# First attention: the value products with their operands exchanged, results by rows and turned back per pair of heads

## The chip, the cores and the metric

The kernel runs on one core of one Trainium2 chip. The metric is the device time of one execution in microseconds. TensorE (PE) multiplies and transposes into PSUM, VectorE (DVE), ScalarE (ACT) and GpSimd (POOL) work element by element, and SyncE (SP) issues the transfers. Each engine runs its own instructions in order; between engines there are semaphores.

## What is computed

The program computes two transformer blocks for 1024 rows of width 1024. The change is in the attention of the first block, which breaks a stick for each query instead of taking a softmax. Cut to what matters:

```python
def stick_breaking_attention(q, k, v):          # 16 heads of 64 columns
    for i in range(seq // Q_BLOCK):             # 8 blocks of 128 queries
        q0, kend = i * Q_BLOCK, (i + 1) * Q_BLOCK
        z = einsum('bhqd,bhkd->bhqk', q[q0:kend], k[:kend]) * inv_sqrt_d
        mask = kpos < qpos
        log_beta = log_sigmoid(z)
        log_1m_beta = where(mask, log_beta - z, 0.0)
        suffix = lax.cumsum(log_1m_beta, axis=3, reverse=True) - log_1m_beta
        a = where(mask, exp(log_beta + suffix), 0.0)
        outs.append(einsum('bhqk,bhkd->bhqd', a, v[:kend]))
...
    o = o.transpose(0, 2, 1, 3).reshape(b, s, D_ATTN)
    o = o * jax.nn.silu(z)                      # the gate
    return x + gate[:, None, :] * (o @ w_out)
```

Everything is fp32. Large products and the scores are made from high and low parts rounded to fp32r; the transposes and the products of `a` with the values are plain fp32.

## The kernel before

The work of the first attention is 128 items, 16 heads times 8 query blocks, in the order 6, 7, 0, 1, 4, 5, 2, 3 of blocks within each head (`STICK_ORDER`). Item n with query block i has i+1 key blocks, so its tiles are up to 1024 wide. The engines pass items on at fixed distances; the loops over steps are written out for each engine (`stick_pe` L748, `stick_act` L984, `stick_dve` L1103, `stick_pool` L1580):

- TensorE makes the scores of item n (L764, L765, two passes of fp32r for every 512 columns, and the mask at L767) in PSUM banks 0 to 3.
- ScalarE takes the sigmoid into `beta` (L994) and the sigmoid of the negative in place (L996), VectorE scans that product from the right into `rest` (L1120, a tile of `M` or `rest`), POOL multiplies the two (L1601): that is `a`, queries by keys, in `beta`.
- Four steps later (`TURN_LAG`) TensorE turns `a` block by block (L779) in pieces of up to four blocks, alternately in PSUM banks 4 and 5; a piece waits for the copy of the piece two places before it. ScalarE copies each piece into `a_T` (L1008), after the two sigmoids of its step. `a_T[i // 2]` holds two items, i-1 and i, side by side.
- Seven steps later (`VALUE_LAG`) come the value products (L801). The values of one head are stationary, 128 keys by 128 columns, of which the 64 columns of the other head of the pair are zero; the moving operand is `a_T`, for both items of a couple at once, 256 columns, and 128 in the last block. So only the odd items have value products, and these are halved over two steps (`part`). The result stands columns by queries, for both heads of a pair, in banks 6 and 7: the zeros let the second head add to the first.
- After an odd head VectorE multiplies each half of 512 queries with the gate `sz` into `s_o` (L1110), and POOL rounds it to the two parts of `opA` (L1587, L1590) for the next product, units from `U_BOUT`.
- SP loads per head its keys and queries (`hin`) and its 64 columns of values (`head_v`, L1348). POOL zeroes the other columns once (L1577).

What decides when a transposed piece may go on:

```python
c = STICK_PLACE[n, p]
if c >= 2:
    pe.wait_ge(act_done, at("stick_hi", c - 2))
```

Of the kernel before, what the change touches and what calls it, by code (L numbers as in the profile page):

```python
# [16 lines left out]
P = 128  # L17
# [118 lines left out]

TURN_LAG, VALUE_LAG, OUT_LAG = 4, 7, 9
BETAS, FACTORS = 5, 3
# [40 lines left out]
STICK_PIECES = stick_pieces()  # L179
STICK_PLACE = {piece: c for c, piece in enumerate(STICK_PIECES)}  # L180

# [111 lines left out]
def program(nc, a, out, known):  # L293
# [3 lines left out]
    with ctx:  # L297
# [10 lines left out]
        def at(name, offset, shape, dt=F32):  # L308
            return nc.alloc_sbuf_tensor_at(name, [P] + shape, dt, offset=offset)
# [36 lines left out]
               [at("a_T3", AT_X + 16 * KIB, [4, 2 * P]), at("a_T3b", AT_X + 20 * KIB, [4, 2 * P])]]  # L346
        head_v = [at(f"head_v{i}", AT_B + (44 + 16 * i) * KIB, [T]) for i in range(2)]
        s_o = at("s_o", AT_M + 12 * KIB, [2, HALF])
        ident_r = at("ident_r", AT_M + 16 * KIB, [P], F32R)
        mask_r = at("mask_r", AT_M + 16 * KIB + 512, [P], F32R)  # L350
# [383 lines left out]

        def stick_kbs(c):
            n, p = STICK_PIECES[c]
            return range(NQ * p, min(NQ * p + NQ, stick_item(n)[1] + 1))
# [10 lines left out]
        def stick_pe(pe):  # L748
            def scores(n):
# [20 lines left out]
                step(pe_done, "stick_s", n)  # L770

            def turn(n):
                pe.wait_ge(pool_done, at("stick_a", n))
                for p in range(stick_item(n)[1] // NQ + 1):
                    c = STICK_PLACE[n, p]
                    if c >= 2:
                        pe.wait_ge(act_done, at("stick_hi", c - 2))
                    for kb in stick_kbs(c):
# [3 lines left out]
                    step(pe_done, "stick_T", c)  # L782

            def values(n, part):

                h, i = stick_item(n)
                s, o = h % 2, 6 + i // NQ
                q0 = (i - 1) % NQ * P
                middle = (i + 1) // 2 - (i > NQ)

                if part == 0:
                    if n % NT == 1:
                        pe.wait_ge(value_in[s], at("value_in", h))
                    if n == 1:
                        pe.wait_ge(pool_done, at("head_zero"))
                    pe.wait_ge(act_done, at("stick_hi", STICK_PLACE[n, i // NQ]))
                    if h >= 2 and h % 2 == 0 and i in (1, NT - 1):
                        pe.wait_ge(dve_done, at("stick_o", h // 2 - 1, i // NQ))
                for kb in range(i + 1)[slice(middle, None) if part else slice(0, middle)]:
                    cols_of = slice(P if kb == i else 0, 2 * P)  # L800
                    ins = pe.matmul(PS[:, o, q0 + cols_of.start:q0 + 2 * P], head_v[s][:, kb * P:(kb + 1) * P],  # L801
                                    a_T[i // 2][kb // NQ][:, kb % NQ, cols_of],
                                    start=(h % 2 == 0 and i in (1, NT - 1) and kb == 0), stop=(h % 2 == 1 and kb == i),
                                    skip_group_check=True)
                if part:
                    ins.then_inc(pe_done, 1)
                    step(pe_done, "stick_v", n)
# [4 lines left out]
            for n in range(STICK_ITEMS + VALUE_LAG + 1):  # L812
                if n < STICK_ITEMS:
                    scores(n)
                if n > VALUE_LAG:
                    part = (n - VALUE_LAG) % 2 == 0
                    values(n - VALUE_LAG - part, part)
# [166 lines left out]
        def stick_act(act):  # L984
            for n in range(STICK_ITEMS + OUT_LAG + 1):
                if n < STICK_ITEMS:
                    w = (stick_item(n)[1] + 1) * P
                    z = stick_z(n)
                    act.wait_ge(pe_done, at("stick_s", n))
                    if n == 0:  # L990
                        act.wait_ge(x_out, at("x_out", 0))
                    if n >= BETAS:
                        act.wait_ge(pe_done, at("stick_T", STICK_PLACE[n - BETAS, stick_item(n - BETAS)[1] // NQ]))
                    act.activation(beta[n % BETAS][:, 0:w], z, ACT.Sigmoid).then_inc(act_done, 1)  # L994
                    step(act_done, "stick_beta", n)
                    act.activation(z, z, ACT.Sigmoid, scale=-1.0).then_inc(act_done, 1)  # L996
                    step(act_done, "stick_rest", n)
                m = n - TURN_LAG
                if 0 <= m < STICK_ITEMS:
                    for p in range(stick_item(m)[1] // NQ + 1):  # L1000
                        c = STICK_PLACE[m, p]
                        kbs = stick_kbs(c)
                        act.wait_ge(pe_done, at("stick_T", c))
                        if m >= NT:
                            act.wait_ge(pe_done, at("stick_v", (m - NT) | 1))
# [3 lines left out]
                        step(act_done, "stick_hi", c)  # L1009

# [92 lines left out]
        def stick_dve(dve):  # L1103
            def finish(j, hf, n):

                dve.wait_ge(pe_done, at("stick_v", n))
                dve.wait_ge(reader(U_BOUT - 1), at("free", U_BOUT - 1))
                if j:
                    dve.wait_ge(pool_done, at("stick_out", j - 1, hf))
                dve.tensor_tensor(s_o[:, hf, :], PS[:, 6 + hf, :], sz[:, j, hf * HALF:(hf + 1) * HALF],  # L1110
                                  ALU.mult).then_inc(dve_done, 1)
                step(dve_done, "stick_o", j, hf)

            for n in range(STICK_ITEMS + OUT_LAG + 1):
                if n < STICK_ITEMS:
# [134 lines left out]
        def _(sp):  # L1250
# [73 lines left out]
            def head_loads(h):  # L1324
# [20 lines left out]
                if h >= 2:  # L1345
                    sp.wait_ge(pe_done, at("stick_v", NT * (h - 1) - 1))
                parts_of = "p (b s d) -> p b s d"
                sp.dma_start(head_v[s][:].rearrange(parts_of, b=NT, s=2)[:, :, s, :],  # L1348
                             v_dram[h // 2].rearrange(parts_of, b=NT, s=2)[:, :, s, :]).then_inc(value_in[h % 2], 16)
                step(value_in[h % 2], "value_in", h, by=16)  # L1350

# [153 lines left out]
        def _(pool):  # L1505
# [46 lines left out]
            def stick_consts():  # L1552
# [16 lines left out]
                step(pool_done, "stick_consts")  # L1569
                for u in (U_QZ + KC - 1, U_QZ + KC - 2):  # L1570
                    pool.wait_ge(stored[u % 2], at("stored", u))
                for u in (U_KV + 2 * KC - 1, U_KV + 2 * KC - 2):
                    pool.wait_ge(v_stored[u % 2], at("v_stored", u))
                for e in range(2):
                    other = head_v[e][:].rearrange("p (b s d) -> p b s d", b=NT, s=2)[:, :, 1 - e, :]
                    pool.wait_ge(pool_done, now(pool_done))
                    pool.memset(other, 0.0).then_inc(pool_done, 1)  # L1577
                    step(pool_done, "head_zero")

            def stick_pool():  # L1580
# [13 lines left out]

                for n in range(STICK_ITEMS + OUT_LAG + 1):
                    if n < STICK_ITEMS:
# [5 lines left out]
                        step(pool_done, "stick_a", n)  # L1602
                    e = n - OUT_LAG
                    if 0 <= e < STICK_ITEMS and e % NT in (5, 7) and e // NT % 2:
                        finish(e // NT // 2, stick_item(e)[1] // NQ)

# [1601 lines left out]
```

## Time and profile before

| | us |
|---|---|
| median of 3 runs | 2759.29 (2758.49 to 2763.61) |
| the profiled execution, own time | 2765.38 |
| its span, first to last instruction | 2763.6 |
| TensorE busy in the span | 2596.2 |
| first attention, first scores to last value product | some 930 to 1211 |

TensorE records are its passes. Their ends are modelled and overlap, so the distance between starts tells what a pass costs. PEld are weight loads. In the timeline one row can hold several equal instructions (x6); its length goes from the first start to the last end. "[0.33 <-PE PS L767]" is idle time before the row and what ended it.

### The profile page before, as it was taken

To read this page: it belongs to the slowest core of one execution; us is meant where nothing else is said; L and a number is where in the kernel's file an instruction comes from. 1 tells how busy PE (TensorE), PEld (TensorE's weight loads), DVE (VectorE), ACT (ScalarE), POOL (GpSimd) and SP (SyncE) were. 2 spreads that over 40 slices of the span, in tenths; PEclk is the share of its full clock that TensorE was granted. 3 is DMA by queue.
4 is the path that set the end of the run, shared out by engine and by line. 5 is a ranking of instruction groups with operands and counts; after the bars stand their busy time and mean duration, and the time that the engine had idled before them with its cause. 6 is when DMAs were issued, how large, how long until landed. Compare 5 with 4: busy or idle time off the path is not lost.

```text
span 2763.6 us, 34691 instructions
## 1 busy us (share of the span) xinstructions
PE 2596.2 (94%) x12363; PEld 2160.0 (78%) x12363; DVE 1548.8 (56%) x2099; ACT 1110.7 (40%) x1866; POOL 855.5 (31%) x626
## 2 busy tenths in 40 slices
PE   3899999999999999999899998789997999999998
PEld 2688888788778799987788877678875888887887
DVE  5666665641325466657764437775568777771112
ACT  3400001431411488856643437661265555551000
POOL 1233332012233466630132220233102323225664
PEclk7999999999999999999999999999999999999999
DMA  5244444344166544434253337414242333339933
GB/s 217 82 147 138 137 137 122 98 155 135 69 230 193 139 111 110 111 116 151 84 183 130 107 125 178 157 44 168 77 145 76 107 107 107 122 98 301 295 91 123
DMA packets 377272, 374.81 MB, mean 136 GB/s; under 512 B 36323, under 2 KB 284556, under 8 KB 376972
## 3 DMA queue, kind: packets, MB, share of 16 engines
q1 hardware_dynamic: 346844, 303.91, 37.0%
q10 hardware_dynamic: 30256, 68.69, 6.6%
q8 instruction: 99, 1.62, 0.2%
q14 instruction: 73, 0.60, 0.1%
HBM read 286.55 MB, written 85.98 MB: 135 GB/s over the span
## 4 chain that ended last, share of the span: by engine, by line
PE 75%; DVE 13%; ACT 5%; DMA 4%; issue 1%; POOL 1%; SPq 0%; ACTq 0%; DVEq 0%; POOLq 0%
PE PS L1743 27%; PE PS L1828 22%; PE PS L1897 8%; PE PS L801 5%; PE PS L779 2%; DMA mod_raw<-in_w_ada 2%; PE PS L1810 2%; PE PS L1787 1%; PE PS L765 1%; PE PS L764 1%; DVE opBf L2938 1%; DVE M L2599 1%; PE PS L1942 1%; DVE prob L1176 1%; ACT opBf L2085 1%
## 5 line engine op out<-in xcount | busy, mean ns | idle before, releaser
L1743 PE MATMUL PS<-opA,w_hi 128*128 128x512 f32 x2240 | 703.9, 394 | 12.2 <-POOL w_lo L1549 5.9
L1743 PEld LDWEIGHTS PS<-opA,w_hi 128*128 128x128 f32 x2240 | 425.2, 190 | 102.9 <-issue 7.3
L1743 PE MATMUL PS<-opA,w_lo 128*128 128x512 f32 x1120 | 439.8, 393 | 0.0
L1544 POOL CAST w_hi<-w_raw 128x1024 fp32r<-128x1024 f32 (+1 forms) x118 | 123.0, 1043 | 770.0 <-PE PS L1743 450.7
L1828 PE MATMUL PS<-opB,Xr 128*128 128x512 f32 x1120 | 308.7, 393 | 15.9 <-ACT M L2264 15.3
L1549 POOL TENSOR_TENSOR w_lo<-w_raw,w_hi 128x1024 fp32r<-128x1024 f32 (+1 forms) x120 | 290.8, 2424 | 83.6 <-ACT w_hi L2144 74.1
L1828 PE MATMUL PS<-opA,Xr 128*128 128x512 f32 x980 | 279.0, 395 | 6.5 <-DVE M L2955 3.4
L2599 DVE SCALAR_TENSOR_TENSOR M<-mod_raw,small,M 128x512 f32<-128x512 f32 x168 | 175.2, 1043 | 169.9 <-DMA mod_raw<-in_w_ada 85.3
L1828 PEld LDWEIGHTS PS<-opB,Xr 128*128 128x128 f32 x1120 | 212.1, 190 | 62.2 <-ACT M L2264 16.6
L1743 PEld LDWEIGHTS PS<-opA,w_lo 128*128 128x128 f32 x1120 | 212.6, 190 | 44.1 <-issue 0.2
L1828 PEld LDWEIGHTS PS<-opA,Xr 128*128 128x128 f32 x980 | 184.0, 190 | 51.1 <-ACT M L2264 8.0
L2881 DVE SCALAR_TENSOR_TENSOR X<-PS,mod,X 128x512 f32<-128x512 f32 x64 | 48.0, 750 | 296.8 <-PE PS L1897 207.1
L1828 PE MATMUL PS<-opA,w_first 128*128 128x512 f32 x840 | 198.0, 392 | 7.4 <-ACT M L2274 7.4
L1828 PEld LDWEIGHTS PS<-opA,w_first 128*128 128x128 f32 x840 | 158.9, 189 | 41.0 <-ACT M L2274 7.8
L1717 POOL TENSOR_TENSOR X<-w_raw 128x512 f32<-128x512 f32 x36 | 48.4, 1345 | 382.8 <-DVE xn L2669 229.3
L1743 PE MATMUL PS<-opB,w_hi 128*128 128x512 f32 x512 | 159.9, 391 | 2.4 <-DVE opB L2869 1.4
L1120 DVE TENSOR_TENSOR_SCAN M<-PS,beta 128x896 f32<-128x896 f32 (+7 forms) x86 | 116.4, 1359 | 71.3 <-ACT PS L996 59.8
L2955 DVE TENSOR_TENSOR M<-M,PS 128x512 f32<-128x512 f32 x140 | 96.2, 687 | 100.5 <-ACT M L2264 65.2
L2919 DVE TENSOR_TENSOR Xr<-X,Xr 128x512 fp32r<-128x512 f32 x140 | 116.0, 829 | 63.3 <-ACT Xr L2236 55.3
L1897 PE MATMUL PS<-opA,w_hi 128*128 128x512 f32 x480 | 149.3, 389 | 0.0
L2158 ACT ACTIVATE squares<-X 128x512 f32<-128x512 f32 x48 | 30.4, 633 | 232.1 <-DVE X L2881 228.4
L2264 ACT ACTIVATE M<-PS 128x512 f32<-128x512 f32 x105 | 62.8, 598 | 151.3 <-PE PS L1828 132.5
(256 smaller groups left out, 4737.7 us busy)
## 6 DMA issues: line engine op xcount, KB each, us to landing
mod_raw<-in_w_ada SPq DMA_DIRECT2D x96, 256.0 KB, 2.9
z_dram<-opB ACTq DMA_DIRECT2D x44, 512.0 KB, 3.9
w_raw<-in_a_w_in SPq DMA_DIRECT2D x32, 512.0 KB, 4.9
hin<-q_dram SPq DMA_DIRECT2D x64, 256.0 KB, 5.8
w_raw<-in_w_down SPq DMA_DIRECT2D x32, 512.0 KB, 4.2
opA<-z_dram SPq DMA_DIRECT2D x60, 256.0 KB, 5.2
mod_raw<-in_b_mod_w SPq DMA_DIRECT2D x48, 256.0 KB, 2.8
X<-x_dram SPq DMA_DIRECT2D x24, 512.0 KB, 6.2
```

The source lines that it names most:

```text
L779: ins = pe.transpose(PS[:, 4 + c % 2, (kb - NQ * p) * P:(kb - NQ * p + 1) * P], beta[n % BETAS][:, kb * P:(kb + 1) * P], ident[:])
L801: ins = pe.matmul(PS[:, o, q0 + cols_of.start:q0 + 2 * P], head_v[s][:, kb * P:(kb + 1) * P], a_T[i // 2][kb // NQ][:, kb % NQ, cols_of], ...
L1120: dve.tensor_tensor_scan(rest[n % FACTORS][:, 0:w][:, ::-1], stick_z(n)[:, ::-1], beta[n % BETAS][:, 0:w][:, ::-1], 1.0, ALU.mult, ALU.byp ...
L1544: pool.tensor_copy(hi, raw).then_inc(pool_done, 1)
L1549: pool.tensor_tensor(lo, raw, hi.bitcast(F32), ALU.subtract).then_inc(pool_done, 1)
L1743: ins = pe.matmul(ps, w[:, k0 + k, :], rhs(part, k0 + k), start=(k == 0 and n == 0), stop=(k == chunks - 1 and n == 2))
L1828: ins = pe.matmul(PS[:, seven_bank(i, which), :], seven_weight(q, i, which, w)[:, c * P:(c + 1) * P], token_part(which, part, c), start=(s ...
L1897: ins = pe.matmul(PS[:, down_bank(hf, n), :], w[:, s, k, :], z_operand(hf, g, part, k), start=(g == 0 and k == 0 and m == 0), stop=(g == 2 ...
L2264: act.activation(block_tile(q, i, 1)[:, 0:HALF] if n == 2 else M[1][:, n * HALF:(n + 1) * HALF], PS[:, seven_bank(i, P1), :], ACT.Copy).th ...
L2599: dve.scalar_tensor_tensor(out=acc, in0=mod_raw[:, n % 2, :], scalar=c, in1=acc, op0=ALU.mult, op1=ALU.add).then_inc(dve_done, 1)
L2919: dve.tensor_tensor(seven_weight(q, i, which, 1), seven_source(i, which), seven_weight(q, i, which, 0).bitcast(F32), ALU.subtract).then_in ...
L2955: dve.tensor_tensor(tile[:, hf * HALF:(hf + 1) * HALF], former, PS[:, seven_bank(i, which), :], ALU.add).then_inc(dve_done, 1)
```

## The change

- The value products exchange their operands (L801 before, L830 after): the turned weights of one item, 128 keys by 128 queries, are stationary, and the 64 value columns of the head move. Every item has its own products, i+1 of them, in one step at the lag of 7. The result stands queries by columns in bank 6 for the even head and bank 7 for the odd, 64 columns for each query block.
- The values need no zeros: they are loaded for two heads at once into `pair_v`, and POOL's two memsets go.
- After each head VectorE copies its bank into `rows_o` (L1150, `ROWS_LAG` 8). After an odd head TensorE turns the pair back (`turn_back`, L842, `BACK_LAG` 9): four transposes for the upper half of the queries, and in the next step four for the lower half. These take places in the rotation of banks 4 and 5 (`STICK_TURNS`), so `turn_free` makes the piece two places behind them wait for VectorE.
- VectorE's gate product then reads bank 4 or 5 (L1158) and comes at `OUT_LAG` 10 and 11, behind the scan of that step; POOL's output follows at the same lag. The loops run one step longer.

```diff
-TURN_LAG, VALUE_LAG, OUT_LAG = 4, 7, 9
+TURN_LAG, VALUE_LAG, ROWS_LAG, BACK_LAG, OUT_LAG = 4, 7, 8, 9, 10
...
+def pair_done(t, lag):
+
+    for hf in (1, 0):
+        h = head_done(t - lag - (1 - hf))
+        if h is not None and h % 2:
+            return h // 2, hf
+    return None
+
+def stick_turns():
+
+    turns = []
+    for t in range(STICK_ITEMS + OUT_LAG + 2):
+        n = t - TURN_LAG
+        if 0 <= n < STICK_ITEMS:
+            turns += [("a", n, p) for p in range(stick_item(n)[1] // NQ + 1)]
+        if pair_done(t, BACK_LAG):
+            turns.append(("o",) + pair_done(t, BACK_LAG))
+    return turns
...
+            def turn_free(c):
+
+                if c >= 2 and STICK_TURNS[c - 2][0] == "o":
+                    pe.wait_ge(dve_done, at("stick_o", *STICK_TURNS[c - 2][1:]))
+                elif c >= 2:
+                    pe.wait_ge(act_done, at("stick_hi", *STICK_TURNS[c - 2][1:]))
...
-                for kb in range(i + 1)[slice(middle, None) if part else slice(0, middle)]:
-                    cols_of = slice(P if kb == i else 0, 2 * P)
-                    ins = pe.matmul(PS[:, o, q0 + cols_of.start:q0 + 2 * P], head_v[s][:, kb * P:(kb + 1) * P],
-                                    a_T[i // 2][kb // NQ][:, kb % NQ, cols_of],
...
+                if h >= 2 and n % NT == 0:
+                    pe.wait_ge(dve_done, at("stick_rows", h - 2))
+                for kb in range(i + 1):
+                    ins = pe.matmul(PS[:, 6 + s, i * DH:(i + 1) * DH],
+                                    a_T[i // 2][kb // NQ][:, kb % NQ, n % 2 * P:n % 2 * P + P],
+                                    pair_v[j % 2][:, kb, s, :], start=(kb == 0), stop=(kb == i), skip_group_check=True)
...
+            def turn_back(j, hf):
+
+                c = STICK_PLACE["o", j, hf]
+                turn_free(c)
+                pe.wait_ge(dve_done, at("stick_rows", 2 * j + 1))
+                for b in range(NQ):
+                    ins = pe.transpose(PS[:, 4 + c % 2, b * P:(b + 1) * P],
+                                       rows_o[:, NQ * hf + b, :, :].rearrange("p s d -> p (s d)"), ident[:])
...
                 if 0 <= n - TURN_LAG < STICK_ITEMS:
                     turn(n - TURN_LAG)
+                if pair_done(n, BACK_LAG):
+                    turn_back(*pair_done(n, BACK_LAG))
...
                     step(dve_done, "stick_scan", n)
-                e = n - OUT_LAG
-                if 0 <= e < STICK_ITEMS and e % NT in (5, 7) and e // NT % 2:
-                    finish(e // NT // 2, stick_item(e)[1] // NQ, e)
+                if head_done(n - ROWS_LAG) is not None:
+                    rows_out(head_done(n - ROWS_LAG))
+                if pair_done(n, OUT_LAG):
+                    finish(*pair_done(n, OUT_LAG))
...
-                sp.dma_start(head_v[s][:].rearrange(parts_of, b=NT, s=2)[:, :, s, :],
-                             v_dram[h // 2].rearrange(parts_of, b=NT, s=2)[:, :, s, :]).then_inc(value_in[h % 2], 16)
+                    sp.dma_start(pair_v[j % 2][:].rearrange("p b s d -> p (b s d)"), v_dram[j]).then_inc(value_in[j % 2], 16)
```

TensorE's rows in step 25, the scores of a head's second item (query block 7), before:

```order
L764 MATMUL PS<-hin 128x512 [waits dve_done]
L765 MATMUL PS<-hin 128x512
L764 MATMUL PS<-hin 128x512
L765 MATMUL PS<-hin 128x512
L767 MATMUL PS<-mask_r,ident_r 128x128
L801 MATMUL PS<-a_T_91,head_v_93 128x256
L801 MATMUL PS<-a_T3b,head_v_93 128x256 x3
L801 MATMUL PS<-a_T3b,head_v_93 128x128
L779 MATMUL PS<-ident,beta_83 128x128 [waits act_done,pool_done]
L779 MATMUL PS<-ident,beta_83 128x128 x3
L779 MATMUL PS<-ident,beta_83 128x128 [waits act_done]
L779 MATMUL PS<-ident,beta_83 128x128
```

and the same step of the changed program:

```order
L794 MATMUL PS<-hin 128x512 [waits dve_done]
L795 MATMUL PS<-hin 128x512
L794 MATMUL PS<-hin 128x512
L795 MATMUL PS<-hin 128x512
L797 MATMUL PS<-mask_r,ident_r 128x128
L830 MATMUL PS<-pair_v_94,a_T_87 128x64 [waits act_done]
L815 MATMUL PS<-ident,beta_83 128x128 [waits act_done,pool_done]
L815 MATMUL PS<-ident,beta_83 128x128 x3
L815 MATMUL PS<-ident,beta_83 128x128 [waits dve_done]
L815 MATMUL PS<-ident,beta_83 128x128
L842 MATMUL PS<-ident,rows_o 128x128 [waits dve_done,act_done]
L842 MATMUL PS<-ident,rows_o 128x128 x3
```

Five value products between the scores and the turn have become one, the second piece of the turn now waits for VectorE (`dve_done`) where it waited for ScalarE's copy, and four transposes back stand behind it. The step before it, with the scores of block 6, ends with the other four.

VectorE's rows around the same step, changed program; the row of 128x1024 is the scan of step 25:

```order
L1168 SCALAR_TENSOR_TENSOR rest_100<-PS,beta_85 128x512 [waits pool_done,act_done]
L1150 COPY rows_o<-PS 128x8x64 [waits dve_done,pe_done]
L1168 SCALAR_TENSOR_TENSOR M_56<-PS,beta_86 128x896 [waits pool_done,act_done]
L1168 SCALAR_TENSOR_TENSOR M_57<-PS,beta_82 128x1024 [waits pool_done,act_done]
L1158 TENSOR_TENSOR s_o<-PS,sz 128x512 [waits dve_done,act_done,pe_done]
L1168 SCALAR_TENSOR_TENSOR rest_100<-PS,beta_83 128x128 [waits pool_done,act_done]
L1158 TENSOR_TENSOR s_o<-PS,sz 128x512 [waits dve_done,act_done,pe_done]
```

Before, the first gate product stood behind the scan of 128x384 and the second behind the one of 128x896, both ahead of the widest; now both stand behind the widest.

## Rows read from the trace of the kernel before

**Rows 1.** The page: busy time of each engine, share of the span, instructions.

```profile
PE 2596.2 (94%) x12363; PEld 2160.0 (78%) x12363; DVE 1548.8 (56%) x2099; ACT 1110.7 (40%) x1866; POOL 855.5 (31%) x626
```

**Rows 2.** Stretches: length, busy per engine, granted clock (1 is full), DMA, GB/s.

```profile
960.00:1200.00 240.00, 240.00 (x1522) 217.52 (x1522) 159.70 (x128) 205.26 (x397) 160.55 (x141) 1.00 0.45 106
```

**Rows 3.** Chain that ended last, 920 to 1240 us: shares, then start and length.

```profile
by line: PE PS L801 40.9%; PE PS L779 19.6%; PE PS L1743 11.4%; PE PS L765 10.7%; PE PS L764 10.4%; PE PS L767 2.8%; DVE M L1120 1.3%; DVE rest L1120 0.6%; ACT beta L994 0.5%; PE PS L1942 0.5%; ACT PS L996 0.5%; issue 0.4%; ACT L994 0.4%; A
...
1051.31 2.00 PE PS L801 x10
...
1060.82 0.87 PE PS L779 x8
...
1068.33 2.00 PE PS L801 x10
```

**Rows 4.** Who waited for whom, 960 to 1200 us: total us, times, longest.

```profile
DVE M L1120 <- ACT PS L996: 43.1, 55, 1.3
```

**Rows 5.** Timeline inside one head: start and length us, engine, line.

```profile
1063.20 0.39 PE L765 MATMUL PS<-hin 128*128 128x512 f32 x1
...
1063.43 0.22 PE L767 MATMUL PS<-mask_r,ident_r 128*128 128x128 f32 x1
...
1063.49 0.87 PE L801 MATMUL PS<-a_T,head_v 128*128 128x256 f32 x4
...
1065.30 1.51 PE L801 MATMUL PS<-a_T,head_v 128*128 128x256 f32 x6
...
1066.64 0.71 PE L779 MATMUL PS<-ident,beta 128*128 128x128 f32 x5
...
1067.28 0.60 ACT L1008 ACTIVATE a_T<-PS 128x512 f32<-128x512 f32 x1
...
1068.11 0.22 PE L767 MATMUL PS<-mask_r,ident_r 128*128 128x128 f32 x1
...
1068.37 1.02 ACT L994 ACTIVATE beta<-PS 128x1024 f32<-128x1024 f32 x1 [0.33 <-PE PS L767]
...
1069.29 1.02 ACT L996 ACTIVATE PS<-PS 128x1024 f32<-128x1024 f32 x1
...
1070.34 2.29 DVE L1120 TENSOR_TENSOR_SCAN rest<-PS,beta 128x1024 f32<-128x1024 f32 x1 [1.06 <-ACT PS L996]
...
1072.22 0.44 PE L801 MATMUL PS<-a_T,head_v 128*128 128x128 f32 x2
...
1072.49 0.60 PE L779 MATMUL PS<-ident,beta 128*128 128x128 f32 x4
```

**Rows 6.** TensorE's timeline where it turns over short passes.

```profile
919.65 1.81 PE L1942 MATMUL PS<-ones,M 128*128 128x1 f32 x15
921.32 0.48 PE L1743 MATMUL PS<-opA,w_hi 128*128 128x512 f32 x1
...
1799.79 1.06 PE L924 MATMUL PS<-aT,vals 128*128 128x128 f32 x8
1800.68 0.71 PE L884 MATMUL PS<-ident,prob 128*128 128x128 f32 x5
```

**Rows 7.** The gate product and POOL's output: nanoseconds least/median/most, first and last start.

```profile
L1110 DVE TENSOR_TENSOR s_o<-PS,sz x16: 662/665/692, 979.0 to 1210.9; 128x512 f32<-128x512 f32 x16
L1587 POOL CAST opA<-s_o x16: 609/610/612, 980.2 to 1212.2; 128x512 fp32r<-128x512 f32 x16
L1590 POOL TENSOR_TENSOR opA<-s_o,opA x16: 1267/1277/1290, 980.9 to 1212.9; 128x512 fp32r<-128x512 f32 x16
```

**Rows 8.** Waits of TensorE and the granted clock beside them.

```profile
1853.80:1857.40 3.60, 3.56 (x13) 3.18 (x14) 0.98 (x3) 2.03 (x4) 0.47 (x1) 0.53 0.00 0
...
1853.84 1.10 PE L884 MATMUL PS<-ident,prob 128*128 128x128 f32 x4 [2.73 <-ACT d_o L1071]
...
935.70:942.50 6.80, 5.52 (x23) 5.08 (x23) 3.67 (x4) 3.72 (x10) 4.67 (x5) 0.50 0.01 3
...
937.04 0.80 PE L764 MATMUL PS<-hin 128*128 128x512 f32 x1 [1.28 <-DVE M L1120]
```

More of the change, by code:

```diff
@@ L179, with head_done @@
 STICK_PIECES = stick_pieces()
-STICK_PLACE = {piece: c for c, piece in enumerate(STICK_PIECES)}
+def head_done(e):
+    return e // NT if 0 <= e < STICK_ITEMS and e % NT == NT - 1 else None
+def pair_done(t, lag):
[13 more added lines that the diff above has]
+    return turns
+STICK_TURNS = stick_turns()
+STICK_PLACE = {turn: c for c, turn in enumerate(STICK_TURNS)}
 SWA_STEPS = 2 * SWA_HEADS
@@ L346, in program @@
                [at("a_T3", AT_X + 16 * KIB, [4, 2 * P]), at("a_T3b", AT_X + 20 * KIB, [4, 2 * P])]]
-        head_v = [at(f"head_v{i}", AT_B + (44 + 16 * i) * KIB, [T]) for i in range(2)]
+        pair_v = [at(f"pair_v{i}", AT_B + (44 + 16 * i) * KIB, [NT, 2, DH]) for i in range(2)]
         s_o = at("s_o", AT_M + 12 * KIB, [2, HALF])
+        rows_o = at("rows_o", AT_M + 12 * KIB, [NT, 2, DH])
         ident_r = at("ident_r", AT_M + 16 * KIB, [P], F32R)
@@ L774, in turn @@
                 for p in range(stick_item(n)[1] // NQ + 1):
[L775 to L778, printed above, removed]
+                    c = STICK_PLACE["a", n, p]
+                    turn_free(c)
+                    for kb in stick_kbs(n, p):
                         ins = pe.transpose(PS[:, 4 + c % 2, (kb - NQ * p) * P:(kb - NQ * p + 1) * P],
@@ L781, in turn, with values @@
                     ins.then_inc(pe_done, 1)
-                    step(pe_done, "stick_T", c)
-            def values(n, part):
+                    step(pe_done, "stick_T", n, p)
+            def values(n):
                 h, i = stick_item(n)
[L787 to L798, printed above, removed]
-                for kb in range(i + 1)[slice(middle, None) if part else slice(0, middle)]:
-                    cols_of = slice(P if kb == i else 0, 2 * P)
-                    ins = pe.matmul(PS[:, o, q0 + cols_of.start:q0 + 2 * P], head_v[s][:, kb * P:(kb + 1) * P],
-                                    a_T[i // 2][kb // NQ][:, kb % NQ, cols_of],
[L803 to L807, printed above, removed]
@@ new lines, in values @@
+                ins.then_inc(pe_done, 1)
+                step(pe_done, "stick_v", n)
+            def turn_back(j, hf):
+                c = STICK_PLACE["o", j, hf]
+                turn_free(c)
+                pe.wait_ge(dve_done, at("stick_rows", 2 * j + 1))
+                for b in range(NQ):
+                    ins = pe.transpose(PS[:, 4 + c % 2, b * P:(b + 1) * P],
+                                       rows_o[:, NQ * hf + b, :, :].rearrange("p s d -> p (s d)"), ident[:])
+                ins.then_inc(pe_done, 1)
+                step(pe_done, "stick_back", j, hf)
@@ L811, in stick_pe @@
             pe.wait_ge(act_done, at("v_hi", U_QZ - 1))
-            for n in range(STICK_ITEMS + VALUE_LAG + 1):
+            for n in range(STICK_ITEMS + OUT_LAG + 2):
                 if n < STICK_ITEMS:
                     scores(n)
-                if n > VALUE_LAG:
-                    part = (n - VALUE_LAG) % 2 == 0
-                    values(n - VALUE_LAG - part, part)
+                if 0 <= n - VALUE_LAG < STICK_ITEMS:
+                    values(n - VALUE_LAG)
                 if 0 <= n - TURN_LAG < STICK_ITEMS:
                     turn(n - TURN_LAG)
+                if pair_done(n, BACK_LAG):
+                    turn_back(*pair_done(n, BACK_LAG))
         def piece_width(x, p):
@@ L984, in stick_act @@
         def stick_act(act):
-            for n in range(STICK_ITEMS + OUT_LAG + 1):
+            for n in range(STICK_ITEMS + OUT_LAG + 2):
                 if n < STICK_ITEMS:
@@ L1008, in stick_act @@
                         act.activation(dst, src, ACT.Copy).then_inc(act_done, 1)
-                        step(act_done, "stick_hi", c)
+                        step(act_done, "stick_hi", m, p)
         def second_act(act):
@@ L1103, in stick_dve, with rows_out, finish @@
         def stick_dve(dve):
-            def finish(j, hf, n):
-                dve.wait_ge(pe_done, at("stick_v", n))
+            def rows_out(h):
+                j, s = divmod(h, 2)
+                dve.wait_ge(pe_done, at("stick_v", NT * h + NT - 1))
+                if j:
+                    dve.wait_ge(pool_done, at("stick_out", j - 1, 0))
+                dve.wait_ge(dve_done, now(dve_done))
+                dve.tensor_copy(rows_o[:, :, s, :], PS[:, 6 + s, :].rearrange("p (b d) -> p b d", d=DH)).then_inc(dve_done, 1)
+                step(dve_done, "stick_rows", h)
+            def finish(j, hf):
+                dve.wait_ge(pe_done, at("stick_back", j, hf))
                 dve.wait_ge(reader(U_BOUT - 1), at("free", U_BOUT - 1))
-                if j:
-                    dve.wait_ge(pool_done, at("stick_out", j - 1, hf))
-                dve.tensor_tensor(s_o[:, hf, :], PS[:, 6 + hf, :], sz[:, j, hf * HALF:(hf + 1) * HALF],
+                dve.wait_ge(dve_done, now(dve_done))
+                dve.tensor_tensor(s_o[:, hf, :], PS[:, 4 + STICK_PLACE["o", j, hf] % 2, :], sz[:, j, hf * HALF:(hf + 1) * HALF],
                                   ALU.mult).then_inc(dve_done, 1)
                 step(dve_done, "stick_o", j, hf)
-            for n in range(STICK_ITEMS + OUT_LAG + 1):
+            for n in range(STICK_ITEMS + OUT_LAG + 2):
                 if n < STICK_ITEMS:
@@ L1344, in head_loads @@
                         step(head_in[h % 2], "head_in", h, by=16)
[L1345 to L1350 removed]
+                if h % 2 == 0:
+                    j = h // 2
+                    if j >= 2:
+                        sp.wait_ge(pe_done, at("stick_v", 2 * NT * (j - 1) - 1))
+                    sp.dma_start(pair_v[j % 2][:].rearrange("p b s d -> p (b s d)"), v_dram[j]).then_inc(value_in[j % 2], 16)
+                    step(value_in[j % 2], "value_in", j, by=16)
             def spill_half(q, hf):
@@ L1569, in stick_consts @@
                 step(pool_done, "stick_consts")
[L1570 to L1578, printed above, removed]
             def stick_pool():
@@ L1593, in finish @@
                     names[("h_att", j, hf)] = names[("stick_out", j, hf)]
-                for n in range(STICK_ITEMS + OUT_LAG + 1):
+                for n in range(STICK_ITEMS + OUT_LAG + 2):
                     if n < STICK_ITEMS:
@@ L1602, in stick_pool @@
                         step(pool_done, "stick_a", n)
-                    e = n - OUT_LAG
-                    if 0 <= e < STICK_ITEMS and e % NT in (5, 7) and e // NT % 2:
-                        finish(e // NT // 2, stick_item(e)[1] // NQ)
+                    if pair_done(n, OUT_LAG):
+                        finish(*pair_done(n, OUT_LAG))
             def second_pool():
```

17 lines of the change are left out of this document (10 added, 7 removed).

## The prediction

> **What bounds the kernel now.** I went from the page to the first attention and then to single steps. On the page TensorE is busy 94% of the span, ScalarE 40%, VectorE 56% [rows 1]. In the steady part of the first attention (960 to 1200 us) TensorE is busy all 240.00 us at full clock, ScalarE 205, VectorE 160, POOL 161 [rows 2]: only TensorE's own work counts there, and each wait that the change gives it is paid in full. The chain that ended last says the same: nearly all of it is TensorE, 40.9% of that stretch of 320 us, 130.9 us, on the value products of L801, and the same ten passes come again after 17.02 us, the time of one head [rows 3]. The others wait: VectorE's scans for ScalarE, 43 us on the tile of M alone [rows 4]. ScalarE has 14% to spare, and its and VectorE's latencies decide as soon as TensorE needs something fresh from them.
>
> **What a pass costs.** Every fp32 product stands in the trace as two records, each with its own weight load: the three value products of one half step are the row x6 at 1065.30 [rows 5]. The ends of records overlap, so I read starts. A 256-column pass takes 0.216 us: the six passes from 1065.30 to 1066.64 make 5 x 0.216 + 0.266, with 0.05 lost once as scores hand over to values [rows 5]. Transposes of 128 columns take 0.87 / 8 = 0.109 [rows 3], the last value passes of 128 columns 0.11. And the column sum with **one** moving column takes 0.111 a pass too (15 passes from 919.65 to 921.32), as does the second attention with 128 ((1800.68 - 1799.79) / 8 = 0.111) [rows 6]. What these have in common is a 128-column load per pass.
>
> **Value products.** Before: per head 16 of 256 columns and 4 of 128: 32 x 0.216 + 8 x 0.11 + 8 x 0.05 = 8.19 us, and the chain gives 130.9 / 16 = 8.18 [rows 3]. After: 36 products of 64 columns, 72 passes. The moving columns fall from 4608 to 2304, but the loads rise from 40 to 72. No row has 64 columns. The bounds are 0.058 us, the step from the mask product at 1063.43 to a value product at 1063.49, whose load was under way during a 512-column pass [rows 5], and 0.216. I take 0.111, since the rows on both sides of 64 (1 and 128) agree on it: 72 x 0.111 + 0.39 = 8.4, **0.25 us more per head, 4 us in all**. The columns saved lie behind the loads.
> The Trainium skill has two rules here (TensorE: Matmul & The Clock Gate). Under LDWEIGHTS a load takes its columns over 1.2 GHz, 107 ns for 128, and the trace agrees with 111. Under Back-to-back issue gap a sustained stream of loads and 128-column products runs at some 81 ns a product; this trace has 111 there, and the trace decides.
>
> **Turning back.** 8 transposes per pair of heads, 64 x 0.109 = **7 us** that were not there; nothing hides them on a full TensorE.
>
> **A new wait, in the middle of a turn.** The transposes back take a place in the rotation of PSUM banks 4 and 5. The turn two places later may not write until VectorE has multiplied that bank with the gate. For the upper half of a pair that turn is the second piece of the item with six blocks, one step later, while VectorE makes the product only **behind the scan of that step**, which is the widest (1024). The scan needs scores of the same step. The chain, read off the same step now [rows 5]: mask product 1068.11, sigmoid 1068.37, second sigmoid 1069.29 to 1070.31, scan 1070.34 to 1072.63, then the product, 0.665 us [rows 7], and some 0.1 for handovers: 1073.4. In front of the wait TensorE has only the item with one block (2 passes, 0.27, as 1072.22 to 1072.49 [rows 5]) and four transposes, 0.44: it is there at 1068.11 + 0.06 + 0.71 = 1068.9. It waits **4.5 us**, for 7 of 8 pairs (the last has no turn behind it): 31.5 us. Queued behind it: the rest of the turn, the other transposes back, all later scores, and through them ScalarE and VectorE.
>
> **Two smaller ones.** The first turning back stands right behind a two-piece turn and needs the bank of its first piece: ScalarE starts that copy 0.3 after the fourth transpose (1066.64 + 3 x 0.109, copy at 1067.28, 0.60 long [rows 5]), so to 1067.9, where TensorE is ready at 1067.2: 0.7 x 7 = 4.9. And the work in a step is no longer levelled: the odd item's values used to be spread over two steps, now the step of the eight-block scores has 2 value passes and the next 4. The three-block turn after them needs the copy of the six-block item's first piece, which on ScalarE stands behind two sigmoids of 1024: mask product + 0.26 + 0.92 + 0.95 + 0.60, at 2.7; TensorE comes at 0.06 + 0.27 + 0.65 + 0.37 + 0.5 = 1.85. The wait is 0.9 in the 8 heads without the large one (there the copy is long made): 7.2.
>
> **Hidden or gone.** The end: the last rows must go PSUM, SBUF and back before turning, VectorE's copy of 512 (0.67 by the product of that size [rows 7]) and handovers, 1 us in which TensorE has nothing. POOL then casts and subtracts both halves of the last pair, 2 x (0.61 + 1.28) = 3.8 [rows 7], from some 0.5 after TensorE has left; unit U_BOUT needs the lower half at its last chunk, 21 passes of 512 columns later (0.23 each, 1063.20 to 1063.43 [rows 5]: 4.8), so 0, and up to 1 if that is off. VectorE gets 16 copies, 12 us on an engine with a third free. POOL's two memsets go from in front of its first `a`, which waits for the first scan in any case: 0. Value loads become 8 whole instead of 16 strided halves, asked for a head or more ahead: 0.
>
> **Clock.** A wait of 2.73 us at 1851 was followed by 3.6 us at a granted 0.53, TensorE busy 3.56 of them: half speed, 1.2 GHz, costs 1.7 us [rows 8]. An idle of 1.28 at the stage's start lies in 6.8 us at 0.50, 5.52 busy: 2.8 us [rows 8]. A wait of 4.5 right behind 0.7 should do as much; I take 1.7 x 7 = 12, with 0 and 20 as ends.
>
> **Sum:** 4 + 7 + 31.5 + 4.9 + 7.2 + 1 = 55.6, with the clock 67.6. The profiled execution (2765.4) would become 2833; it is 6 above the median, so from 2759.3: **2827 us**.
>
> **Rivals.**
> - *The clock holds.* The large waits are some 40 us apart, all between full stretches. 2815. Against: the row at 1851. 0.12.
> - *The clock stays down.* 64-column passes leave the array idle half of each 0.111 us, so low stretches may not end soon. At 4 us a stall instead of 1.7 it is 2843; beyond that up to some 2900. 0.08.
> - *The bank is free in time* (ScalarE and VectorE run further ahead than I read, or the wait is met by the earlier step): without 31.5 and the clock 2783. The order of VectorE's rows speaks against it. 0.03.
> - *Loads come closer than 0.111.* Half way between 0.058 and 0.111, at 0.085 a pass, it is 1152 x 0.026 = 30 less: 2797. The rows at 1 and 128 columns speak against it. 0.03. By the rate under Back-to-back issue gap, on the page of the Trainium skill named above, it would be 1152 x 0.030 = 35 less, 2792.
> - *Faster.* If a 64-column pass costs what it streams, values are 72 x 0.058 + 0.39 = 4.6 us a head, 58 less. Against that 7 for turning back and 44.6 for waits leave -6: 2753, if the clock holds. It decides from 0.063 us a pass down (16 x (8.19 - 0.39 - 72p) = 51.6). For it: the 0.058 row; against: that row's load was hidden by a long pass, and here all passes are short. 0.03.
> - *No change*, some mixture of these: 0.02.
>
> **Numbers.** The forecast case has 0.69 and reaches from 2812 to 2850. A measurement of this kernel can tell about 0.2%, 5.5 us, from no change. The range 2800 to 2856 takes in the steady clock and most of the low one, and leaves out some 0.15. Faster 0.03, same 0.02, slower 0.95.
>
> **What would show it.** Passes of 64 columns 0.111 apart; the value line at some 8.4 us a head; 7 waits of 4 to 5 us of TensorE for VectorE's gate product, each in front of the last two transposes of a turn; waits of about 0.9 and 0.7 for ScalarE's copies; a head pair taking 40 us and more against 34.0; granted clock near 0.5 for some us after each large wait. I am wrong if these passes stand well under 0.1 apart, if the gate product ends before TensorE gets there, or if the first attention grows by less than 40 us.

## The result and the profile after

The changed kernel takes **2854.72 us** (median of 4 runs, 2841.76 to 2868.07) against 2761.45 before (4 runs), a ratio of 1.034 with a 95% interval of 1.027 to 1.040: 93 us slower. Measured once more, beside the first experiments, it was 2844.52 against 2766.21, 1.028 (1.026 to 1.030), 78 us. The profiled execution of the first measurement is its fastest run, 2841.76; its span of 2840.0 us is 76.4 longer than that of before.

TensorE's busy share hardly moves on the page (94% before, 93% after); the first attention shows the difference. The two stretches go from the first scores to the start of the next unit, before and after (columns as in [rows 2]):

```profile
929.80:1210.60 280.80, 275.81 (x1729) 249.29 (x1729) 180.52 (x143) 234.97 (x450) 181.39 (x159) 0.99 0.43 101
```
```profile
928.10:1286.50 358.40, 308.52 (x2305) 294.26 (x2305) 192.59 (x159) 235.46 (x450) 180.77 (x158) 0.91 0.33 80
```

That is 77.6 us more, so the whole difference of the profiles lies here; the rest of the span is 2482.8 us before and 2481.6 after. TensorE is busy 32.7 us longer and idle 44.9 us longer, and its mean granted clock falls from 0.99 to 0.91. What it waited for, 960 to 1290 us:

```profile
PE PS L815 <- DVE s_o L1158: 31.6, 7, 4.5
PE PS L815 <- ACT a_T L1047: 7.8, 9, 1.0
PE PS L842 <- ACT a_T L1047: 4.1, 7, 0.6
PE PS L842 <- DVE rows_o L1150: 0.9, 1, 0.9
```

Before there was not one such wait in the steady part [rows 2]. The large one, in the timeline of the changed kernel, once per pair of heads:

```profile
1032.12 0.22 PE L797 MATMUL PS<-mask_r,ident_r 128*128 128x128 f32 x1
...
1032.38 1.02 ACT L1033 ACTIVATE beta<-PS 128x1024 f32<-128x1024 f32 x1 [1.56 <-PE PS L797]
1032.40 0.61 PE L815 MATMUL PS<-ident,beta 128*128 128x128 f32 x4
1033.30 1.02 ACT L1035 ACTIVATE PS<-PS 128x1024 f32<-128x1024 f32 x1
...
1034.35 2.29 DVE L1168 TENSOR_TENSOR_SCAN rest<-PS,beta 128x1024 f32<-128x1024 f32 x1 [2.75 <-ACT PS L1035]
1036.77 0.69 DVE L1158 TENSOR_TENSOR s_o<-PS,sz 128x512 f32<-128x512 f32 x1
...
1037.52 0.69 PE L815 MATMUL PS<-ident,beta 128*128 128x128 f32 x2 [4.51 <-DVE s_o L1158]
```

This is the step of [rows 5] at 1068.11: mask product 1032.12, sigmoids to 1034.32, scan to 1036.64, product to 1037.46, and TensorE, whose fourth transpose ends by its row at 1033.01, goes on at 1037.52, 4.51 later. The passes of 64 columns at full clock:

```profile
1006.88 1.05 PE L830 MATMUL PS<-pair_v,a_T 128*128 128x64 f32 x8
1007.77 0.83 PE L830 MATMUL PS<-pair_v,a_T3b 128*128 128x64 f32 x6
1008.44 0.39 PE L815 MATMUL PS<-ident,beta 128*128 128x128 f32 x2
```

Eight passes from 1006.88 to 1007.77 are 0.111 us each, and the next six, to 1008.44, are too (0.112). And the clock after the seven waits, one row for each low stretch:

```profile
991.00:1001.20 10.20, 9.60 (x45) 9.41 (x45) 2.35 (x4) 3.67 (x9) 6.58 (x7) 0.50 0.01 2
1035.30:1045.60 10.30, 8.08 (x38) 7.89 (x38) 3.84 (x5) 2.58 (x7) 6.72 (x7) 0.50 0.00 2
1083.10:1086.50 3.40, 3.40 (x20) 3.40 (x18) 1.12 (x2) 1.32 (x4) 3.13 (x4) 0.50 0.00 0
1124.10:1134.30 10.20, 8.58 (x40) 8.39 (x40) 3.24 (x5) 2.65 (x8) 6.72 (x7) 0.50 0.01 2
1171.90:1178.70 6.80, 6.80 (x34) 6.61 (x33) 1.81 (x3) 2.30 (x7) 5.24 (x7) 0.50 0.00 0
1216.20:1219.70 3.50, 3.50 (x20) 3.50 (x18) 1.12 (x2) 1.54 (x5) 3.10 (x5) 0.51 0.00 0
1257.20:1267.40 10.20, 8.65 (x40) 8.46 (x41) 3.17 (x5) 2.72 (x8) 6.72 (x7) 0.50 0.01 2
sum 54.60, PE 48.61 PEld 47.65 DVE 16.63 ACT 16.78 POOL 38.20; mean PE 6.94 PEld 6.81 DVE 2.38 ACT 2.40 POOL 5.46
```

### The profile page after: what moved, and what is told of

The parts are those of the page before. It is cut to its first block, busy times and chain, and to the rows that moved or that the text cites. A ratio compares the mean times of both kernels' runs of the same rounds, so it can differ in the third digit from the quotient of the medians.

```text
span 2840.0 us, 35871 instructions
## 1 busy us (share of the span) xinstructions
PE 2627.7 (93%) x12939; PEld 2205.0 (78%) x12939; DVE 1557.9 (55%) x2115; ACT 1111.4 (39%) x1866; POOL 854.8 (30%) x624
## 4 chain that ended last, share of the span: by engine, by line
PE 76%; DVE 12%; ACT 5%; DMA 3%; issue 2%; SPq 1%; POOL 1%; ACTq 0%; DVEq 0%; POOLq 0%
PE PS L1782 27%; PE PS L1867 22%; PE PS L1936 8%; PE PS L830 5%; PE PS L1826 3%; PE PS L815 2%; PE PS L1849 2%; DMA mod_raw<-in_w_ada 1%; PE PS L795 1%; PE PS L794 1%; PE PS L1981 1%; DVE M L2638 1%; DVE prob L1225 1%; PE PS L923 1%; DMA mod_raw<-in_a_mod_w 1%
## 5 line engine op out<-in xcount | busy, mean ns | idle before, releaser
L1641 POOL TENSOR_TENSOR beta<-beta,M 128x895 f32<-128x895 f32 (+7 forms) x86 | 103.5, 1209 | 111.1 <-DVE M L1168 93.0
L815 PE MATMUL PS<-ident,beta 128*128 128x128 f32 x576 | 92.9, 289 | 41.4 <-DVE s_o L1158 31.6
```

Of the source, the lines that this page charges most:

```text
L1641: pool.tensor_tensor(b[:, 0:w - 1], b[:, 0:w - 1], rest[n % FACTORS][:, 1:w], ALU.mult).then_inc(pool_done, 1)
```

## The experiments

The waits and the passes are as forecast, but the clock took more, so the theories to tell apart are about the clock. **Theory N**: passes with 64 columns keep the clock low after a wait. **Theory W**: the wait alone decides how long it is low. Then VectorE's order, the bank of the transposes back and the lag of the value products were changed, each on top of the one before. The first four runs below were made on one chip, beside a before of 2766.21; the last four on another, beside a before of 2764.45.

**The changed kernel once more** (no edit).

> The changed kernel again, beside the experiments on the same chip. Theory N (64-column passes keep the granted clock low for long after each large wait) and theory W (the wait alone decides) both say: 2840 to 2870 us, 7 waits of 4.5 us for the gate product, some 30 to 90 us of the first attention at half clock, and the spread of the runs comes from how long these stretches are.

2844.52 us (2843.67 to 2850.55), first attention 358.2 us in the profile, the same seven waits (31.6 us), and after them low stretches of the same lengths:

```profile
sum 54.40, PE 48.28 PEld 47.32 DVE 16.77 ACT 16.60 POOL 38.27; mean PE 6.90 PEld 6.76 DVE 2.40 ACT 2.37 POOL 5.47
```

"The changed kernel" below is this run; its runs lie closer together than those of the first measurement. Its profiled execution is 8.7 us slower than the first one (2850.55 against 2841.76), and that difference lies outside the first attention: 2490.6 us there instead of 2481.6.

**The gate product ahead of the scan.**

```diff
             for n in range(STICK_ITEMS + OUT_LAG + 2):
+                if pair_done(n, OUT_LAG):
+                    finish(*pair_done(n, OUT_LAG))
                 if n < STICK_ITEMS:
...
                     rows_out(head_done(n - ROWS_LAG))
-                if pair_done(n, OUT_LAG):
-                    finish(*pair_done(n, OUT_LAG))
```

> VectorE makes the gate product ahead of the scan of its step instead of behind it. Both theories: the seven waits of 4.5 us go (31.6 us), no stretch of low clock is left in the first attention, but the second turning back now meets ScalarE's copy behind the two wide sigmoids and waits some 1.8 us in seven places (12 us). Before plus 4 for passes, 7 for turning back, 8 and 17 for ScalarE's copies, 1 at the end: 2761 + 37 = 2798, and the runs lie close together. A rival, that the wait only moves to the scan's other side: more than 2830.

2812.96 us (2811.54 to 2822.06), ratio to before 1.018 (1.015 to 1.020). Two lines in VectorE's order give back 32 us of 78. The stretch of the first attention and the waits of TensorE in it:

```profile
934.40:1253.60 319.20, 289.86 (x2304) 275.82 (x2305) 191.34 (x159) 232.56 (x449) 179.09 (x157) 0.97 0.37 89
...
PE PS L842 <- ACT a_T L1047: 15.7, 14, 1.7
PE PS L815 <- ACT a_T L1047: 8.8, 10, 1.0
```

The seven waits for VectorE are gone. The first attention is 319.2 us, 38.4 over before, where 37 was expected; the whole kernel was 10 us over what was expected in the median (46.8 instead of 37), and in the profile 8 of these lie outside the first attention (span 2810.0 less 319.2 is 2490.8, against 2482.8 before). The changed kernel on this chip has the same there, 2848.8 less 358.2, so the change of this run did not make them. One low stretch of 6.8 us behind the stage's start was left, so "no low clock" was not quite met.

**128 columns move instead of 64** (results land on top of each other).

```diff
-                    ins = pe.matmul(PS[:, 6 + s, i * DH:(i + 1) * DH],
+                    ins = pe.matmul(PS[:, 6 + s, i % NQ * P:(i % NQ + 1) * P],
...
-                                    pair_v[j % 2][:, kb, s, :], start=(kb == 0), stop=(kb == i), skip_group_check=True)
+                                    pair_v[j % 2][:, kb, :, :].rearrange("p s d -> p (s d)"), start=(kb == 0), stop=(kb == i), skip_group_check=True)
```

> All 128 value columns move instead of the 64 of the head (results land in four places of the bank over each other, so the output is not the attention's). If a pass is bound by its load, passes stay 0.111 to 0.112 apart and, at full clock, nothing changes. Theory N: twice the columns keep the array busy, the low stretches after the waits shrink from 54.6 us in the profile to 35 or less, and the median falls by 5 to 20 us. Theory W: low stretches and time as in the changed kernel. Rival that a pass costs its columns: passes 0.107 now and 0.054 with 64, so a time some 60 us longer.

2843.95 us (2839.92 to 2844.96), the same as the changed kernel. Twice the columns for nothing: this shows that a 64-column pass is bound by something other than its columns. The seven low stretches, each of 6.8 us, in sum:

```profile
sum 47.60, PE 36.83 PEld 36.85 DVE 19.41 ACT 13.85 POOL 38.63; mean PE 5.26 PEld 5.26 DVE 2.77 ACT 1.98 POOL 5.52
```

TensorE was busy 36.8 us at half clock instead of 48.3, so 6 us less was lost, as theory N wants, though the stretches shrank to 47.6 us and not to the 35 expected. The gain did not arrive, because the passes were not quite equal:

```profile
1024.22 1.11 PE L830 MATMUL PS<-pair_v,a_T 128*128 128x128 f32 x8
1025.16 0.83 PE L830 MATMUL PS<-pair_v,a_T3b 128*128 128x128 f32 x6
1025.83 0.38 PE L815 MATMUL PS<-ident,beta 128*128 128x128 f32 x2
```

The first eight passes of a step take 0.94 us here (1025.16 - 1024.22) and 0.89 with 64 columns; the six behind them take 0.67 in both, 0.112 each. So the pass itself costs the same, and 0.05 is added once a step, where the scores hand over to the values: over 128 steps 6 us. This run alone does not decide between N and W.

**32 columns move** (half of each result is left out).

```diff
-                    ins = pe.matmul(PS[:, 6 + s, i * DH:(i + 1) * DH],
+                    ins = pe.matmul(PS[:, 6 + s, i * DH:i * DH + 32],
...
-                                    pair_v[j % 2][:, kb, s, :], start=(kb == 0), stop=(kb == i), skip_group_check=True)
+                                    pair_v[j % 2][:, kb, s, 0:32], start=(kb == 0), stop=(kb == i), skip_group_check=True)
```

> Only 32 of the 64 value columns move (half of each result is left out). Load-bound: passes stay 0.111 apart. Theory N: the array is idle more, low stretches grow beyond 55 us, time up by 5 to 40 us over the changed kernel. Theory W: the same as the changed kernel. Rival that a pass costs its columns: some 30 us less.

**2940.40 us** (2932.87 to 2950.58): half the columns, 96 us slower than the changed kernel. At full clock eight passes behind the scores take 0.86 us ((1031.76 - 1030.90) / 8 = 0.1075) and the next group of six 0.112 each, so it is not the passes. It is the clock:

```profile
960.00:1380.00 420.00, 377.74 (x2160) 361.41 (x2159) 177.53 (x148) 219.74 (x417) 167.22 (x147) 0.69 0.25 60
...
1030.90 1.03 PE L830 MATMUL PS<-pair_v,a_T 128*128 128x32 f32 x8
1031.76 0.31 PE L815 MATMUL PS<-ident,beta 128*128 128x128 f32 x1
...
1033.29 0.83 PE L830 MATMUL PS<-pair_v,a_T3b 128*128 128x32 f32 x6
1033.96 0.41 PE L815 MATMUL PS<-ident,beta 128*128 128x128 f32 x2
```

The granted clock is 0.69 on average over 420 us. Theory N expected a rise of 5 to 40 and got 96; theory W, no change, is refuted, and so is the rival by which columns cost time.

**32 columns and no large wait.** The edits of the two runs on the product's place and on 32 columns together.

> 32 value columns move and the gate product stands ahead of the scan, so no wait is longer than 1.7 us (half of each result is left out). Theory N: the array is idle enough for the clock to fall and stay low even without a large wait: over 100 us at half clock in the first attention and 40 us or more over the same kernel with 64 columns (2813). Rival: low clock needs a long wait to begin; then within 5 us of 2813.

2878.48 us (2870.76 to 2883.81), 66 over the same kernel with 64 columns (measured on the other chip; each against its own before, 114.0 and 46.8, it is 67). The first attention, and TensorE's longest waits in it:

```profile
927.40:1315.20 387.80, 359.40 (x2304) 342.10 (x2305) 191.56 (x159) 236.32 (x450) 180.56 (x158) 0.78 0.31 75
...
PE PS L842 <- ACT a_T L1047: 14.8, 14, 1.7
PE PS L794 <- DVE M L1170: 3.5, 2, 2.9
```

The wait of 2.9 us stands at the start of the stage. Behind it no wait is longer than 1.7 us, and the granted clock of 0.78 over 387.8 us still means some 171 us at half clock. In one place the clock was back at full before it fell for 27 us:

```profile
942.00:952.00 10.00, 8.95 (x75) 8.59 (x75) 6.50 (x5) 8.18 (x18) 5.22 (x4) 1.00 0.87 209
952.00:979.00 27.00, 27.00 (x118) 25.84 (x118) 9.28 (x9) 11.45 (x21) 9.54 (x8) 0.50 0.25 60
979.00:996.00 17.00, 16.00 (x133) 15.33 (x131) 10.22 (x9) 13.63 (x27) 7.72 (x7) 0.99 0.25 59
```

In the second row TensorE has passes in flight all 27.00 us and the granted clock is 0.50 throughout. So idle time is not what kept it down there; the kernel with the product ahead of the scan differs in the moving columns alone, and behind the start of the stage it had 6.8 us of low clock in all.

**The kernel before with a wait in the same place.**

```diff
                     if c >= 2:
                         pe.wait_ge(act_done, at("stick_hi", c - 2))
+                    if n > NT and n % (2 * NT) == 5 and p == 1:
+                        pe.wait_ge(pool_done, at("stick_a", n + 4))
```

> The kernel before, with one wait added in the same place: the second piece of the turn of the item with six blocks waits, in seven of the odd heads, until POOL has multiplied the item four steps later. By the chain of the trace of before (scan done 4.6 us after the mask product, 2.2 more for POOL, TensorE there after 2.5) that is 4.2 us a time, 29 us. Theory W (the wait alone sets the length of the low clock): low stretches as in the changed kernel, some 55 us of them, and 24 us lost, so before plus 53. Theory N (narrow passes prolong them): with 256-column passes the stretches are 3.4 to 6.8 us, at most 45 us in all, and before plus 35 to 45.

2815.11 us (2812.46 to 2817.20), before plus 50.7, above N's 35 to 45 and just below W's 53. The wait was longer than I had worked out:

```profile
PE PS L781 <- POOL beta L1603: 32.4, 7, 4.6
...
994.70:998.10 3.40, 3.40 (x15) 3.11 (x16) 0.42 (x1) 1.53 (x5) 0.41 (x1) 0.50 0.00 0
...
1073.20:1080.00 6.80, 4.38 (x20) 4.12 (x20) 0.75 (x2) 1.98 (x6) 2.68 (x3) 0.50 0.05 11
...
sum 40.80, PE 28.68 PEld 26.83 DVE 5.00 ACT 13.17 POOL 14.25; mean PE 4.10 PEld 3.83 DVE 0.71 ACT 1.88 POOL 2.04
```

The waits are 32.4 us, seven of 4.6. To that comes half of 28.7 us busy at half clock, 14.3; the sum is 46.7, and the first attention grew by 47.6 (280.8 to 328.4). With waits as long as in the changed kernel, the wide passes lose 14.3 us to the clock where the 64-column passes lose 24.3. So N is right in kind, and W holds for the larger part of the amount. This kernel also has no transposes back behind the wait; with them and 128 columns it was 18.4, half of 36.83. The three amounts are sums over seven waits in one trace each (48.61 and 48.28 us busy in the two traces of the changed kernel).

**The transposes back in a bank of their own.** Bank 7 is empty between two odd heads. The lower half comes three steps after the upper, VectorE's gate product reads bank 7, and it stands ahead of the scan.

```diff
-        h = head_done(t - lag - (1 - hf))
+        h = head_done(t - lag - 3 * (1 - hf))
...
-        if pair_done(t, BACK_LAG):
-            turns.append(("o",) + pair_done(t, BACK_LAG))
...
                     pe.wait_ge(dve_done, at("stick_rows", h - 2))
+                    if s:
+                        pe.wait_ge(dve_done, at("stick_o", j - 1, 0))
...
-                c = STICK_PLACE["o", j, hf]
-                turn_free(c)
                 pe.wait_ge(dve_done, at("stick_rows", 2 * j + 1))
+                if hf == 0:
+                    pe.wait_ge(dve_done, at("stick_o", j, 1))
                 for b in range(NQ):
-                    ins = pe.transpose(PS[:, 4 + c % 2, b * P:(b + 1) * P],
+                    ins = pe.transpose(PS[:, 7, b * P:(b + 1) * P],
```

> The transposes back go into bank 7, which is empty between the two odd heads, the lower half three steps after the upper, and the gate product stands ahead of the scan: banks 4 and 5 rotate as before. If all large waits come from the shared rotation, only ScalarE's copy after the two wide sigmoids is left (0.9 to 1.0 us in each of 16 heads) and 1 us at the end: passes -1, turning back 7, waits 16: before plus 23, 2784 to 2792, no low clock in the first attention. If the transposes back cost by themselves something else, more than 2800.

2794.91 us (2786.32 to 2798.09, 5 runs), ratio to before 1.011 (1.010 to 1.012), before plus 30 and 3 us above the range expected; the first attention is 306.6 us, plus 25.8 where 23 was expected.

```profile
931.60:1238.20 306.60, 284.41 (x2305) 273.17 (x2305) 191.53 (x159) 232.97 (x450) 180.76 (x160) 0.99 0.40 95
...
PE PS L811 <- ACT a_T L1045: 16.0, 17, 1.0
```

What is left is mainly ScalarE's copy, 17 times, 16.0 us, at a mean clock of 0.99. The transposes back by themselves do no further harm.

**And the value products one step later.** The same kernel with one more line:

```diff
-TURN_LAG, VALUE_LAG, ROWS_LAG, BACK_LAG, OUT_LAG = 4, 7, 8, 9, 10
+TURN_LAG, VALUE_LAG, ROWS_LAG, BACK_LAG, OUT_LAG = 4, 8, 9, 10, 11
```

> As the one before, and the value products one step later (lag 8), so that the 16 passes of the eight-block item stand in the step of the widest scores and TensorE comes to the critical copy at 3.2 us instead of 1.85, after it is made (2.8). If the unlevelled steps are the cause of the remaining waits, these go: before plus 8, 2769 to 2777. If not, no change against the one before.

**2774.09 us** (2768.83 to 2782.56, 6 runs), ratio to before 1.004 (1.003 to 1.006), before plus 10. Of the 16.0 us of waits for ScalarE's copies 0.4 is left:

```profile
926.30:1216.60 290.30, 283.04 (x2303) 272.06 (x2304) 192.47 (x159) 235.88 (x450) 180.38 (x158) 0.99 0.41 99
...
PE PS L840 <- DVE s_o L1156: 0.9, 1, 0.9
PE PS L840 <- DVE rows_o L1148: 0.8, 1, 0.8
PE PS L811 <- ACT a_T L1045: 0.4, 1, 0.4
```

That is 9.5 us over before in the first attention. The shares of the chain there, before and in this kernel:

```profile
by line: PE PS L801 46.5%; PE PS L779 22.3%; PE PS L765 12.2%; PE PS L764 11.9%; PE PS L767 3.2%; DVE M L1120 1.5%; DVE rest L1120 0.6%; ACT beta L994 0.6%; ACT PS L996 0.5%; ACT L994 0.5%; issue 0.1%
```
```profile
by line: PE PS L828 44.0%; PE PS L811 22.3%; PE PS L793 12.0%; PE PS L792 11.8%; PE PS L795 3.2%; PE PS L840 2.5%; DVE M L1168 1.5%; DVE rest L1168 0.6%; ACT beta L1031 0.6%; ACT PS L1033 0.5%; issue 0.4%; DVE s_o L1156 0.2%; DVE rows_o L11
```

Value products 46.5% of 280.8 = 130.6 us, now 44.0% of 290.3 = 127.7; turning back (L840) 2.5% = 7.3 us. So of the 9.5 us, turning back is 7.3, the value passes are 2.9 less, the three groups of waits are 2.1, and some 3 are spread over small pieces that I did not follow. The exchange itself gains 3 us and costs 7. No version of it was faster than the kernel before; this is the best found.

## Why the prediction was right, and where it was off

The prediction, 2827 in a range of 2800 to 2856, has the direction and the mechanism, and the measured 2854.72 lies at the upper edge; the forecast increase was 68 us, the measured one 93 and, measured once more, 78. That the first median fell inside the range is in part luck: it is 1.3 us below the upper end, between two pairs of runs, of which the slower (2865.51 and 2868.07) lies beyond it. The 2844.52 of the second measurement is well inside.

- *A pass of 64 columns is bound by its load, 0.111.* The cost is shown: 0.112 in the second group of a step for 32, 64 and 128 columns alike, with 0.86, 0.89 and 0.94 for the first eight. That the load is what binds it is inferred: it is what these passes and the one-column ones [rows 6] have in common, and no run changed the load.
- *Value products 4 us more.* The terms as written give less, 72 x 0.111 + 0.39 - 8.19 = 0.19 a head and 3 us in all, and the sign is wrong: in the chain of the last experiment they are 2.9 us less. There they take 127.7 / 16 = 7.98 us a head, which is 72 x 0.111 without the 0.39. The 0.05 a handover between scores and values [rows 5] was carried over from wide passes; with 128 columns it is there, with 64 it is not.
- *Turning back, 7 us.* It is 7.3 in the last experiment.
- *The wait for the gate product, 31.5.* It is 31.6, seven times 4.5. That its place behind the scan is the cause is shown by moving it.
- *The two waits for ScalarE, 4.9 and 7.2.* They are 4.1 and 7.8, and the wait at the end is 0.9 for 1. All waits together: 44.4 measured, 44.6 forecast.
- *The clock, 12 us.* This is **the term that was mis-sized**. Half of 48.61 us busy at half clock is 24.3 in the profile, 3.5 a wait instead of 1.7. The step that failed is "a wait of 4.5 right behind 0.7 should do as much" as the wait at 1851 [rows 8]. The low stretches were 3.4 to 10.3 us instead of 3.6. Behind the wait at 1851 stood four transposes and then 512-column passes (first row, before); here stood six transposes, narrow scores and 64-column passes (the last two rows are of the latter, still at half clock):

```profile
1854.60 2.80 PE L864 MATMUL PS<-keys,opA 128*128 128x512 f32 x8
...
1041.42 1.91 PE L830 MATMUL PS<-pair_v,a_T 128*128 128x64 f32 x8
1043.12 0.63 PE L830 MATMUL PS<-pair_v,a_T2b 128*128 128x64 f32 x2
```

The kernel before with the added wait lost 14.3, 2.0 a wait, so for wide passes the 12 was nearly right. The rival "the clock stays down", which I gave 0.08, names the mechanism and with 4 us a stall nearly the size; it should have been the forecast's middle.

- *What the terms leave.* As measured they are 44.4 + 24.3 + 7.3 - 2.9 = 73.1 of the 77.6 us by which the first attention grew. The other 4.5 were not followed up.
- *The rest to the median.* Of the four runs two (2841.76 and 2843.93) have a mean granted clock of 0.966 and 0.967, the other two (2868.07 and 2865.51) 0.958 and 0.959, and the median lies between the pairs. An estimate from these: 0.008 less over 2850 us is 23 us lost, which is the distance of the pairs. Where in the kernel that clock was lost is open. There is no trace of the slower pair, and between the two profiled executions of this kernel the difference lay outside the first attention.

With 24 for 12 the forecast would have been 2839, 16 below the median and 3 below the fastest run.

## What to carry to other kernels

Exchanging the operands to halve the moving columns gains next to nothing (here 3 us of 131) when each pass still needs a 128-column weight load and costs 0.11 us, in plain fp32, whether 32, 64 or 128 columns move; count loads before columns. A tile that joins a rotation of buffers brings its reader's latency into the rotation: look at what that reader's engine does first, and put the reader ahead of the long instruction, or give the tile an idle buffer. On a saturated engine, work per step should stay level, or another engine's latency comes through in the light steps (one step of lag took away 15.6 us of waits here). A wait costs more than its length: price the clock behind it by the passes that follow it, here 3.5 us a wait with 64 columns and 2.0 with 256.

## What the runs showed of the hardware

TensorE's granted clock stayed at 0.50 for 27 us in which its passes followed each other without a gap and the value products moved 32 columns. After the waits of 4.5 us the low stretches were 3.4 to 10.3 us long with 64 columns, 6.8 with 128, and 3.4 to 6.8 with 256, and TensorE worked in them for 3.4 to 9.6, 5.0 to 5.8 and 3.4 to 4.4 us. Moving 32 columns instead of 64 made the kernel 96 us slower (2940 against 2845).

At half clock a pass of one column with its load takes twice as long as at full clock, so the load slows with the clock. The row shows the kernel before near its start, 16 such passes (columns as in [rows 2]):

```profile
62.70:66.20 3.50, 3.50 (x16) 3.46 (x16) 0.00 (x0) 0.00 (x0) 0.00 (x0) 0.50 0.00 0
```

The loads are busy 3.46 us, 0.216 a pass, against 0.111 at full clock [rows 6]. The 64-column passes do the same: eight from 1041.42 to 1043.12 at half clock are 0.2125 each, against 0.111.
